# Four index-weight columns of a mixing block computed with the value projection (260 columns a matmul)

## What is computed

```
z = h @ w_in
uv, pz, qz, kz, vz, qi, ki, wi, cz, gz = split(z, [512, 256, 256, 256, 256, 128, 32, 4, 512, 4096])
# sparse attention, per block of queries:
w_idx = wi * IDX_HEADS ** -0.5                    # 4 heads, so times 0.5
rel = relu(einsum('bqhd,bsd->bqhs', q_idx, k_idx) * IDX_HD ** -0.5)
score = einsum('bqh,bqhs->bqs', w_idx, rel)       # causal, then top_k(score, 64)
...
o = einsum('bqhk,bqkhd->bqhd', p, vs)             # p: softmax over the chosen keys, vs: the values
```

## Time and profile before

| | us |
|---|---|
| median of 3 runs | 2570.84 |
| lowest and highest run | 2569.1, 2571.25 |
| the profiled execution | 2569.46 |
| its span, first to last instruction | 2567.7 |
| TensorE busy (share of the span) | 2464.9 (96%) |
| VectorE busy | 1637.2 (64%) |
| ScalarE busy | 1201.6 (47%) |

### The profile page before, as it was taken

One profiled execution on the slowest core, in us unless ns is written; L12 is line 12 of the kernel. 1 busy time (PEld: TensorE's weight loads), 2 busy tenths in 40 slices (PEclk: granted clock), 3 DMA queues, 4 the chain that ended last, 5 costly groups with the idle time before them and its releaser, 6 DMA issues.

```text
span 2567.7 us, 34302 instructions
## 1 busy us (share of the span) xinstructions
PE 2464.9 (96%) x14089; PEld 2106.6 (82%) x14089; DVE 1637.2 (64%) x2149; ACT 1201.6 (47%) x1441; POOL 214.6 (8%) x334
## 2 busy tenths in 40 slices
PE   7999999999999999899999999999999999998998
PEld 5888998788788899788778888887877879887886
DVE  4776777776776686777667565565555456557544
ACT  4435464433433546444443346944444443694443
POOL 2000002000100000300010000210000000021000
PEclk9999999999999999999999999999999999999999
DMA  8785455786786444678578645455646545445552
GB/s 292 258 284 155 146 169 192 251 294 231 263 287 229 142 148 158 226 266 284 191 265 296 204 143 146 132 167 190 203 156 214 184 160 157 132 132 178 196 186 104
DMA packets 369163, 514.27 MB, mean 200 GB/s; under 512 B 21600, under 2 KB 310614, under 8 KB 369008
## 3 DMA queue, kind: packets, MB, share of 16 engines
q1 hardware_dynamic: 342608, 415.80, 50.0%
q0 software_dynamic: 26400, 96.28, 10.7%
HBM read 510.89 MB, written 1.13 MB: 199 GB/s over the span
## 4 chain that ended last, share of the span: by engine, by line
PE 83%; DVE 8%; ACT 4%; issue 3%; POOL 1%; DMA 0%; SPq 0%; DVEq 0%; POOLq 0%; ACTq 0%
PE ps L1658 76%; DVE lo L1083 3%; ACT hi L708 2%; PE ps L1704 2%; PE ps L1806 1%; PE ps L1680 1%; PE ps L1834 1%; PE ps L1844 1%; DVE arena L1572 1%; POOL T L641 1%; DVE arena L1142 1%; PE ps L1853 1%; DMA raw<-in_ffn_w_gu 0%; ACT arena L748 0%; DVE X L1116 0%
## 5 line engine op out<-in xcount | busy, mean ns | idle before, releaser
L1083 DVE TENSOR_TENSOR lo<-raw,hi 128x2048 fp32r<-128x2048 f32 (+1 forms) x400 | 908.5, 2273 | 579.7 <-ACT hi L708 578.8
L708 ACT ACTIVATE hi<-raw 128x2048 fp32r<-128x2048 f32 (+1 forms) x400 | 757.5, 1897 | 526.4 <-PE ps L1658 511.0
L1658 PE MATMUL ps<-hi,NH 128*128 128x512 f32 (+3 forms) x1760 | 682.5, 388 | 38.4 <-DVE lo L1083 14.8
L1658 PE MATMUL ps<-hi,NL 128*128 128x512 f32 (+3 forms) x1760 | 672.5, 382 | 0.0
L1658 PE MATMUL ps<-lo,NH 128*128 128x512 f32 (+3 forms) x1760 | 672.0, 382 | 0.0
L1658 PEld LDWEIGHTS ps<-hi,NH 128*128 128x128 f32 x1760 | 337.4, 192 | 113.7 <-DVE lo L1083 32.1
L1658 PE MATMUL ps<-NH,hi 128*128 128x256 f32 x1376 | 395.2, 287 | 0.0
L1658 PEld LDWEIGHTS ps<-hi,NL 128*128 128x128 f32 x1760 | 336.5, 191 | 66.7
L1658 PEld LDWEIGHTS ps<-lo,NH 128*128 128x128 f32 x1760 | 337.2, 192 | 63.9
L1658 PE MATMUL ps<-NL,hi 128*128 128x256 f32 x1376 | 388.9, 283 | 0.0
L1658 PE MATMUL ps<-NH,lo 128*128 128x256 f32 x1376 | 387.5, 282 | 0.0
(11 more groups left out here) (297 smaller groups left out, 2043.8 us busy)
## 6 DMA issues: line engine op xcount, KB each, us to landing
raw<-in_ffn_w_gu SPq DMA_DIRECT2D x176, 512.0 KB, 4.9
raw<-in_ffn_w_in SPq DMA_DIRECT2D x176, 512.0 KB, 4.6
arena<-in_ada_w POOLq DMA_DIRECT2D x72, 1024.0 KB, 7.2
raw<-in_w_in SPq DMA_DIRECT2D x96, 512.0 KB, 4.5
raw<-in_ffn_w_down SPq DMA_DIRECT2D x88, 512.0 KB, 4.7
raw<-in_ffn_w_out SPq DMA_DIRECT2D x88, 512.0 KB, 4.1
raw<-in_mix_w_in SPq DMA_DIRECT2D x86, 512.0 KB, 4.5
raw<-in_w_branch SPq DMA_DIRECT2D x16, 512.0 KB, 3.9
```

The costliest lines, as they stand in the source:

```text
L708: last = nc.scalar.activation(dst, src, ACT.Copy)
L1083: last = nc.vector.tensor_tensor(dst, src, part.bitcast(F32), ALU.subtract)
L1658: last = nc.tensor.matmul(dst, a, b, start=start and k == 0, stop=stop and k == 2, skip_group_check=skip)
```

## The change

The four index-weight columns are put behind the 256 value columns of unit 1. Unit 1 is now 260 columns wide: one transfer brings the 256 value columns of all eight chunks, and a second the four index-weight columns (column 1696 on) of all eight. Its matmuls stream 260 columns. Since 2 x 260 floats don't fit one bank, the second half of the tokens goes to bank 3, and the transposes of gm0, which use bank 3 next, wait until unit 1 has been copied out. That copy is four instructions: for each half 256 columns to `VT` and four to `WI`. Unit 6 loses the four columns, its 48 thin matmuls, one small piece of each split, and the copy of eight columns.

```diff
-COLS1 = [..., (1536, 164), (768, 256), (1024, 256)]
+COLS1 = [..., (1536, 160), (768, 256), (1024, 256)]
+VU_N, WI_COLS = T + 4, 1696
...
+                    if u == V_U:
+                        view = i["w_in"][l].rearrange("(c p) n -> p c n", p=P)
+                        load(s.base + u, [(lambda slot, a=a, b=b: cols(slot, a, b, VU_N), view[:, :, o:o + b - a])
+                                          for a, b, o in ((0, T, COLS1[V_U][0]), (T, VU_N, WI_COLS))])
...
             if s.kind == "m" and s.block == 1 and u == IDX_U:
-                        (a[:, :, 128:256].rearrange("p c (k n) -> p c k n", k=4), spread(b[:, :, 128:160], 2, 4)),
-                        (a[:, :, 256:260], b[:, :, 160:164])]
+                        (a[:, :, 128:256].rearrange("p c (k n) -> p c k n", k=4), spread(b[:, :, 128:160], 2, 4))]
+            if s.kind == "m" and s.block == 1 and u == V_U:
+                n = 8 * VU_N
...
+                elif u == V_U:
+                    for t, b in ((0, 1), (1, 3)):
+                        nc.scalar.activation(VT[:, t, :], ps[:, b, 0:T], ACT.Copy)
+                        ins = nc.scalar.activation(WI[:, t, :], ps[:, b, T:VU_N], ACT.Copy, scale=0.5)
...
-                    if u == IDX_U:
-                        ins = nc.scalar.activation(WI.rearrange("p a b -> p (a b)"), ps[:, 7, 0:8], ACT.Copy, scale=0.5)
...
-                if u == IDX_U:
-                    channels(bank[:, 0:T], s, 260, 0)
-                    channels(bank[:, T:2 * T], s, 260, P)
-                    for t in range(2):
-                        last = tokens(ps[:, 7, 4 * t:4 * t + 4], s, 260, T, 4, t)
-                elif u < BR1:
+                if u < BR1:
...
                 if work == "gm0":
+                    pe.wait_ge(act_done, at("act", f"ev {V_U}"))
...
+                    if s.block == 1 and u == V_U:
+                        return tokens(ps[:, (1, 3)[t], 0:VU_N], u, VU_N, 0, VU_N, t, chunks)
```

More of the change, by code:

```diff
@@ L31 @@
 V_GATE, V_U, CONV_A, CONV_G, U_GATE, POOL_U, IDX_U, Q_U, K_U, GATES1, BR1, OUT1 = 0, 1, 2, 3, 4, 5, 6, 7, 8, 9, 25, 29
-COLS1 = [(256, 256), (1280, 256), (1700, 256), (1956, 256), (0, 256), (512, 256), (1536, 164), (768, 256), (1024, 256)]
+COLS1 = [(256, 256), (1280, 256), (1700, 256), (1956, 256), (0, 256), (512, 256), (1536, 160), (768, 256), (1024, 256)]
 COLS1 += [(2212 + 256 * i, 256) for i in range(16)]
+VU_N, WI_COLS = T + 4, 1696
 DV_U, FV_U, NQ_U, KV_U, DQK_U, DVF_U, VG_U, FQK_U, W1_U, GATES2, BR2, OUT2 = 0, 1, 2, 3, 4, 7, 8, 9, 12, 14, 26, 29
@@ L414, in mix1 @@
                 for u in range(UNITS):
-                    if u < BR1:
+                    if u == V_U:
+                        view = i["w_in"][l].rearrange("(c p) n -> p c n", p=P)
+                        load(s.base + u, [(lambda slot, a=a, b=b: cols(slot, a, b, VU_N), view[:, :, o:o + b - a])
+                                          for a, b, o in ((0, T, COLS1[V_U][0]), (T, VU_N, WI_COLS))])
+                    elif u < BR1:
                         load(s.base + u, halves(i["w_in"][l], *COLS1[u]))
@@ L686, in split_pieces @@
             if s.kind == "m" and s.block == 1 and u == IDX_U:
-                a, b = dst[:, slot, 0:8 * 260].rearrange("p (c n) -> p c n", n=260), raw[:, slot, 0:8 * 164].rearrange("p (c n) -> p c n", n=164)
+                a, b = dst[:, slot, 0:2048].rearrange("p (c n) -> p c n", n=T), raw[:, slot, 0:8 * 160].rearrange("p (c n) -> p c n", n=160)
                 return [(a[:, :, 0:128], b[:, :, 0:128]),
-                        (a[:, :, 128:256].rearrange("p c (k n) -> p c k n", k=4), spread(b[:, :, 128:160], 2, 4)),
-                        (a[:, :, 256:260], b[:, :, 160:164])]
+                        (a[:, :, 128:256].rearrange("p c (k n) -> p c k n", k=4), spread(b[:, :, 128:160], 2, 4))]
             n = 2048
+            if s.kind == "m" and s.block == 1 and u == V_U:
+                n = 8 * VU_N
             if s.kind == "m" and s.block == 2 and u == VG_U:
@@ L863, in evac1 @@
                     ins = nc.scalar.activation(PZ[:, :, 16:16 + T], bank.rearrange("p (a t) -> p a t", a=2), ACT.Copy)
-                elif u in (Q_U, K_U, V_U, IDX_U, CONV_A):
-                    dst = {Q_U: QT, K_U: KT, V_U: VT, IDX_U: QKI, CONV_A: CA}[u]
+                elif u == V_U:
+                    for t, b in ((0, 1), (1, 3)):
+                        nc.scalar.activation(VT[:, t, :], ps[:, b, 0:T], ACT.Copy)
+                        ins = nc.scalar.activation(WI[:, t, :], ps[:, b, T:VU_N], ACT.Copy, scale=0.5)
+                elif u in (Q_U, K_U, IDX_U, CONV_A):
+                    dst = {Q_U: QT, K_U: KT, IDX_U: QKI, CONV_A: CA}[u]
                     ins = nc.scalar.activation(dst, bank.rearrange("p (a t) -> p a t", a=2), ACT.Copy)
-                    if u == IDX_U:
-                        ins = nc.scalar.activation(WI.rearrange("p a b -> p (a b)"), ps[:, 7, 0:8], ACT.Copy, scale=0.5)
                 elif u == CONV_G:
```

## The result

The changed kernel took 2550.88 us (median of 4 runs, 2546.65 to 2552.42), the kernel before 2571.05 us beside it (median of 4, 2569.1 to 2572.24). The ratio is 0.992, with a 95% interval of 0.9902 to 0.9937: 16 to 25 us gained. The profiled execution of after took 2550.27 us, against 2569.46 before, 19.19 us less. A second measurement gave 2546.72 against 2570.73 us (experiment e5).

The account below looks back on a forecast made before the run. TensorE's matmuls, 83% of the chain, were taken as the bound. -18.62 + 2 x (0.07 + 0.06) = -18.36 us took 2569.46 to 2551.1, plus 1.4 for a median: 2552.5 us, range 2549 to 2557.

Parts of the forecast that it names:

- The removal, -18.62 us: Units 6 and 7, both layers: dropping thin matmuls saves 10.5 us of their own and 8.1 us of low clock.
- 260 columns, 2.9 ns a matmul: Unit 1 on TensorE: four extra columns add 2.9 ns to each of 24 unhidden matmuls, 0.07 us a layer.
- The split, 0.06 us a layer: Unit 1's split on ScalarE and VectorE, ahead of the norm: 32 more elements cost 33 and 30 ns.
- Evacuation, 0.94 to 1.54 us: Copying out unit 1: four copies together take this long, and gm0's wait for them costs nothing.
- The load: Unit 1's transfers, one in 16-byte pieces: at most 8.2 us, inside 20.1 us of room, so no cost.
- What is late next: After unit 7: pooling ends 0.3 us before TensorE's small matmul, and VectorE's full stretch starts 8.5 us earlier.
- B: Rival: VectorE's full stretch doesn't move, so only 4.3 us a layer are gained; 2562.5 us, chance 0.05.
- A: Rival: the clock falls in units 6 and 7 anyway, so only 10.2 us are gained; 2560.6 us, chance 0.06.
- C: Rival: thin pieces make unit 1's load land late and the kernel slower; 2582 us at 35 us landing, chance 0.03.
- D: Rival: other clock falls, behind waits at stage ends, get longer or shorter; 2555 to 2558 us if bad, chance 0.06.
- The forecast: Whole kernel: 18 us gained, 2550 to 2555 us, likeliest 2552.5 us, chance 0.80.
- The sign that I had set myself: Stage from first norm to merge: the forecast is wrong if not 8 to 10 us shorter in each layer.

Follow-up runs that it names:

- e5: The changed kernel as it is, measured a second time; 2546.72 us against 2570.73 for the kernel before.
- e1: Kernel before without its 48 thin matmuls a layer, index weights left out, none of the change's additions; 2548.15 us against 2564.83.
- e4: Kernel before with the same thin matmuls in unit 6, three after every three wide ones instead of all at its end; 2562.2 us against 2564.83.
- e3: Kernel before with each of the 48 thin matmuls streaming 128 columns instead of 4; 2562.94 us against 2564.83.
- e10: Kernel before, thin matmuls kept, plus unread matmuls in TensorE's waits at stage starts and before block 2's decay sums; 2553.21 us, ratio 0.9944.
- e11: Kernel before with each of the 48 thin matmuls streaming 64 columns instead of 4; 2566.01 us against 2569.74.
- e6: Kernel before plus all that the change adds (wider unit 1, transfers, split, copies, gm0's wait), unit 6 unchanged; 2568.15 us against 2570.73.

## Why the prediction was right

**The removal, -18.62 us.** Right, in size and in cause. The two stretches are 18.80 us shorter in after and 18.58 in e1. The split into a price of the matmuls (10.5) and of the clock (8.1) nearly holds as well: e4 and e3, which keep the 48 matmuls and lose the fall, are 7.8 and 7.9 us shorter than before in the two stretches, and after is another 11.0 us shorter than e4.

**260 columns, 2.9 ns a matmul.** 0.1209 - 0.1177 = 3.2 ns; 24 of them are 0.08 us a layer, predicted 0.07.

**The split, 0.06 us a layer.** Right, 0.07, once it is read between two marks. The transposes after the norm start 0.46 us later than before (232.94 against 232.48), but they do so in e1 as well, whose split has its old length: in both kernels the work ahead of the split had already slipped, by 0.39 us in after and 0.46 in e1. From the start of the split of unit 1 to the transposes it is 232.94 - 222.58 = 10.36 us in after, 232.48 - 222.19 = 10.29 before, and 10.29 in e1 (222.65 to 232.94).

**Evacuation, 0.94 to 1.54 us.** Mis-sized: 0.80 us. I had added up four durations, and the floor of that sum was already too high, since a copy starts before the one ahead of it has ended (243.21 against 242.93 + 0.38). It changed nothing: gm0 waits for nothing, as said.

**The load.** Right: 5.4 and 5.3 us, inside the bound of 8.2 and the room of 20.1.

**What is late next.** The cover of 0.3 us by which pooling would be ahead of the small matmul was 0.2 us, and no wait came. VectorE's full stretch moved by 7.7 us with TensorE; B is out. The 8.5 us that I had put for this move was the gain of the stretch itself (8.57 us by the chain); the marks ahead of it had slipped by 0.87 us (267.01 against 266.14), of which 0.08 and 0.07 us are the additions; e1, without them, had slipped by 0.74.

**The rivals.** A fell with e1, B by the rows of after, C by the load's 5.3 us. D was there, more than its 0.06 said, though on the good side: the medians differ by 20.2 us against my 18.4, and the second measurement of after, 2546.72 us, lies under my range of 2549 to 2557. In the profiles the other falls moved by more than the 0.4 us that is left in the sum. How much earlier after reaches the same instruction on VectorE, in us:

| mark | before | after | earlier by |
|---|---|---|---|
| norm ahead of layer 1's mixing | 226.35 | 226.80 | -0.45 |
| gating ahead of its merge | 398.66 | 390.95 | 7.71 |
| its result added to `X` | 438.83 | 430.13 | 8.70 |
| norm ahead of layer 2's mixing | 852.31 | 845.03 | 7.28 |
| gating ahead of its merge | 1027.22 | 1009.01 | 18.21 |
| its result added to `X` | 1067.22 | 1048.22 | 19.00 |

Between 398.66 and 438.83 before has a fall that after lacks, and between 438.83 and 852.31 after has one that before lacks. Both pairs of rows below are the same wait of TensorE, each in before and then in after:

```profile
426.53 0.73 PE L1658 MATMUL ps<-hi,NH 128*128 128x512 f32 x1 [2.72 <-DVE NL L1584]
418.82 0.47 PE L1667 MATMUL ps<-hi,NH 128*128 128x512 f32 x1 [2.71 <-DVE NL L1593]
...
656.87 0.50 PE L1658 MATMUL ps<-hi,NH 128*128 128x512 f32 x1 [2.36 <-DVE lo L1083]
648.20 0.50 PE L1667 MATMUL ps<-hi,NH 128*128 128x512 f32 x1 [2.37 <-DVE lo L1092]
```

```profile
424.00:428.00 4.00, 1.47 (x4) 1.22 (x5) 2.76 (x5) 3.30 (x4) 1.32 (x2) 0.82 0.69 220
648.00:652.00 4.00, 3.80 (x16) 3.27 (x17) 2.49 (x6) 0.91 (x2) 2.49 (x5) 0.71 0.61 187
```

The clock falls at the first in before (0.82) and not in after (1.00 from 416 to 424), and at the second in after (0.71) and not in before (1.00 from 656 to 664). Waits of the same length did it in one kernel's profile and not in the other's; what decides it, no run here shows. That these moves cancelled to 0.4 us is luck. Five microseconds between two executions of one kernel, by falls of the clock elsewhere, are what the range should have allowed on both sides. The first measurement, 2550.88, lies in it.

**The forecast.** 2552.5 us against 2550.88. The missing 1.6 us is not in any term of the sum, whose stretch was measured to 0.2 us. It is of the size of one fall more or less, but no run shows that it is one. The chances as written add up to 0.97 for a faster kernel, not 0.96; nothing hangs on it.

**The sign that I had set myself.** The stage from the norm to the merge was to be 8 to 10 us shorter in each layer. From the norm to the gating in the table it is 8.16 us shorter in layer 1 and 10.93 in layer 2; this is layer 2, before and then after:

```profile
852.31 1.28 DVE L1106 SCALAR_TENSOR_TENSOR arena<-ps,arena 128x512 f32<-128x512 f32 x2
1027.22 2.48 DVE L1572 TENSOR_TENSOR arena<-arena,ps 128x512 f32<-128x512 f32 x4
...
845.03 1.28 DVE L1115 SCALAR_TENSOR_TENSOR arena<-ps,arena 128x512 f32<-128x512 f32 x2
1009.01 2.48 DVE L1581 TENSOR_TENSOR arena<-arena,ps 128x512 f32<-128x512 f32 x4
```

So layer 2 missed this sign by 0.9 us, on the good side. Units 6 and 7 give 10.23 of the 10.93 us, which alone is over 10 (for this layer I had 10.14 us of gain, so the upper bound was too tight). The other 0.7 us lie at the stage's start, where the clock is low after the wait for the norm in both kernels: from the transposes after the norm to unit 3 it is 875.03 - 858.44 = 16.59 us before and 867.04 - 851.16 = 15.88 after. The sum had no term for that.

## What to carry to other kernels

Look at the granted clock of every stretch of matmuls, not only at TensorE's busy time, which was 100% through both falls here. A block of 48 matmuls of four columns cost 5.3 us of its own and another 3 to 5 us in what came after it. If the thin operand shares the standing side with a wide one, append its columns to that; if it can't, spreading the thin ones among wide ones (e4), or widening them (e3), kept the clock at 1.00 without removing anything. Those experiments won 7.8 us in units 6 and 7, of which the medians of the whole kernel showed 2 to 3. Where TensorE has to wait at a stage's start, a few matmuls that nobody reads, fewer than the wait can hold, were worth 10 us in this kernel; where no wait covered them they cost their full price.

## What the runs showed of the hardware

- A matmul of 128 x 128 standing weights took 0.1095 us with 4 columns, 0.1106 with 128, 0.1177 with 256 and 0.1209 with 260: from 4 to 128 columns the price hardly rises. Every one of them has new standing weights; no run here has the same ones twice, so whether these set the price isn't shown.
- A gapless run of 48 matmuls of 4 columns brought the clock from 2.4 to 1.2 GHz even where it had been 1.00 since the stage's start (e10); 64 columns still did, for less time; 128 and 256 didn't; nor did 4 columns alternated three and three with 256.
- The cost of a fall came in like pieces: units 6 and 7 took 16.9 us without one (e3), 18.4 (e10, e11), 20.0 and 21.6 us with one, 1.5 to 1.6 us apart. Both profiles of before have 20.0 in layer 1 and 21.6 in layer 2, e6 has 21.6 in both.
- A wait of TensorE of 2.4 to 2.7 us was followed by a low clock in one profile and by 1.00 in another, with the same work around it.
- The same program differs by up to 10 us from run to run, with its mean granted clock. Single profiles can be compared stretch by stretch, hardly by their whole time when a few microseconds matter.
